# An encoder trunk in fp32 on one core: the next block's projections inside the attention units, conv groups between blocks, rotary halves swapped by DMA, 64-row scores

## The chip, the core and the metric

The kernel runs on one core of one Trainium2 chip. The metric is the device time of one launch in microseconds (us); lower is better. The engines are named as in the profile: PE (matrix engine; PEld is its weight load), DVE (vector engine), ACT (scalar engine), POOL (GpSimd), SP (the engine that issues most transfers).

## The reference

Two layers of an encoder on 1280 tokens (1024 of one sequence, 256 of another), 1024 wide. Each layer normalises its input, multiplies by `w_in`, and splits the 3072 result columns among three mixers. Their outputs together go through `w_out`, a norm and the residual; then a SwiGLU feed-forward network (2816 wide) with the same norms.

```python
hn = rmsnorm(x, g_pre_mix)
q_d, k_d, v_d, q_n, k_n, v_n, gate_b, gate_c, h_in = split(hn @ w_in)
y_dil  = dilated_attention(rope(q_d), rope(k_d), v_d)       # 6 heads of 64
y_na   = neighbourhood_attention(q_n, k_n, v_n, rpb)        # 4 heads of 64
y_conv = gate_b * conv3(gate_c * h_in)                      # 384 channels
x = x + rmsnorm(concat(y_dil, y_na, y_conv) @ w_out, g_post_mix)
hf = rmsnorm(x, g_pre_ffn)
x = x + rmsnorm((silu(hf @ w_gate) * (hf @ w_up)) @ w_down, g_post_ffn)
```

The three (window, dilation) pairs of the dilated attention are one softmax over all keys with the logarithm of a count added to the scores.

## The kernel before

**Precision.** Every product of two fp32 matrices is three matmuls on a high and a low part: high x high, high x low, low x high (`products`, L1617 to L1619). The high part is an ACT copy (`WH`, `XH`), the low part a subtraction on POOL (`WL`, L653) or DVE (`XL`).

**Tiling.** Activations lie transposed, features on the partitions, tokens in three chunks `c` of 512, 512 and 256 columns. A *group* is one 128-column slice of a weight matrix times one chunk: 8 k-tiles x 3 matmuls into one PSUM bank. A *weight unit* is that slice for all three chunks, such as `("k", 1)`.

**Attention blocks.** A block `b` holds two heads of 64, stacked in 128 partitions. Blocks 0 to 2 are dilated, 3 and 4 neighbourhood attention. Each has 20 *attention units* `u` (10 query tiles of 128 x 2 heads). The keys of a unit are 8 tiles (u 0 to 15) or 2 tiles (u 16 to 19) in dilated blocks, and 4, 5 or 2 tiles in the others. A unit passes through: `scores` on PE (L1730, L1731), `mask` on DVE (L1344: adds the table and gives the row maximum), `exp` on ACT (L921), `turn` on PE (L1742: transposes of the probabilities), their high part on ACT (`PTH`, L953) and low part on DVE (`PTL`, L1377), `values` on PE (L1763, L1764), `o_low` on ACT (`OT`, L931), `normalise` on DVE (`YN`, L1353), and for each second unit `turn_y` on PE (L1770) with `y_block` on ACT. Every engine works its instructions in the order in which they are written.

**Order around a block.** PE works the nine groups k, q, v of block `b`, then in blocks 0 to 2 the three `c` groups of the convolution; scores(0) and scores(1); `turn_v` (L1711: transposes of v); then the 20 units. In blocks 0 to 2 the `h` and `b` groups of the convolution are spread over units 0 to 11 (`convolution`). While PE works the projections, ACT and DVE make rotary embedding and the split into stacked halves.

**Rotary embedding.** `swap` on ACT copies four 32-row pieces of the group from PSUM to the exchanged place; DVE multiplies by sine and adds.

**Scores.** The contraction dimension is 64 per head. `QS[h]` holds the high part of q in one half of the 128 partitions and the low part in the other, `KH[h]` the high part of k twice. One 128-row matmul of `QS` with `KH` gives high x high and low x high, a second with `KL` the rest:

```python
nc.tensor.matmul(bank, q, KH[h][:, keys], start=True, stop=False)
last = nc.tensor.matmul(bank, q, KL[h][:, keys], start=False, stop=True)
```

**Banks.** Two results `o` of values use one bank (6) in dilated blocks and two (6 and 7, `out_banks`) in the others.

Of the kernel before, what the change touches and what calls it, by code (L numbers as in the profile page):

```python
# [54 lines left out]
MIXED_PIECES = ((0, 2), (2, 4), (5, 7), (7, 8))  # L55
VBANKS = ((6, 0, 4), (7, 4, 4), (6, 8, 2))
SUM_BANK = 7
CONV_PARTS = ((0, S_SAMPLE, 1), (S_SAMPLE, S_PROMPT, S_SAMPLE + 2))
# [40 lines left out]

def attention_weights(L):  # L100

    order = []
    for b in range(BLOCKS):
        order += [(L, part, b) for part in "kqv"]
        if b in DIL:
            order += [(L, part, b) for part in "chb"]
    return order + [(L, "o", i) for i in range(KT)]
# [19 lines left out]
NSLOT = 10  # L127
SPLIT = Numbered(WEIGHTS)
# [11 lines left out]


def conv_groups(L, b, parts):
    return [(L, part, b, c) for part in parts for c in range(NCH)]
# [21 lines left out]
def groups():  # L165
    order = first_block(0)
    for L in range(DEPTH):
        for b in range(BLOCKS):
            if b:
                order += [(L, part, b, c) for part in "kqv" for c in range(NCH)]  # L170
            if b in DIL:
                order += conv_groups(L, b, "chb")
# [23 lines left out]
def drains():  # L196
    order = []
    for L in range(DEPTH):
        for b in range(BLOCKS):
            order += first_block(L) if b == 0 else [(L, p, b, c) for p in "kqv" for c in range(NCH)]  # L200
            if b in DIL:
                order += conv_groups(L, b, "chb")
    return order
# [4 lines left out]
SWAP, SINE, ROPE = Numbered(ROPED), Numbered(ROPED), Numbered(ROPED)  # L208


def splits():

    order = []
    for L in range(DEPTH):
        for b in range(BLOCKS):
            if b == 0:
                order += [(L, p, b, c) for c in range(NCH) for p in "kq"]
            else:
                order += [(L, p, b, c) for p in "kq" for c in range(NCH)]
    return order  # L220


STACK_HI, STACK_LO = Numbered(splits()), Numbered(splits())


# [56 lines left out]
ON_VECTOR = [(2 * L + 1, "x", 0) for L in range(DEPTH - 1)]  # L282
# [14 lines left out]
def constants():  # L297
# [14 lines left out]
    eye_ones = np.concatenate([np.eye(P, dtype=f), np.ones((P, P), f), cmask], 1)  # L312
    return np.ascontiguousarray(np.concatenate([cos128, sin128, log], 1)), eye_ones


def build(nc, xt, w_in, w_out, w_gate, w_up, w_down, gains, conv_w, rpb, tables, small, mixed,
          parked, out):
    with ExitStack() as ctx:
# [19 lines left out]
        EYE = place("EYE", [P, 2 * P + GRID_W])  # L338
        ident, ones, cmask = EYE[:, 0:P], EYE[:, P:2 * P], EYE[:, 2 * P:]
# [9 lines left out]
                [base + o for o in (91136, 57344, 65536, 73728, 32768)]  # L349
# [5 lines left out]
        QS = [place(f"QS{h}", [P, T], F32R, offset=base + 5120 * h) for h in range(2)]  # L355
        KH = [place(f"KH{h}", [P, T], F32R, offset=base + 10240 + 5120 * h) for h in range(2)]
        KL = [place(f"KL{h}", [P, T], F32R, offset=base + 20480 + 5120 * h) for h in range(2)]
        V = place("V", [P, TILES, 2, P], F32R, offset=base + 30720)
        PR = place("PR", [P, 2, 1024], offset=base + 40960)
        pt = (w_at + 4 * 8192, base + 49152)  # L360
        PTH = [place(f"PTH{i}", [P, 2, 4, P], F32R, offset=o) for i, o in enumerate(pt)]
        PTL = [place(f"PTL{i}", [P, 2, 4, P], F32R, offset=o + 4096) for i, o in enumerate(pt)]
        TA = place("TA", [P, T + 4], offset=base + 57344)
        TB = place("TB", [P, T + 4], offset=base + 62496)
        TC = place("TC", [P, T + 4], offset=base + 67648)
        YB = place("YB", [P, T], offset=base + 72800)
        TAB = place("TAB", [P, 2 * T + 1920], offset=base + 77920)
        COS, SIN, LOG = TAB[:, 0:T], TAB[:, T:2 * T], TAB[:, 2 * T:]
        EB = place("EB", [P, 2, 14, GRID_W], offset=base + 77920)
        IB = place("IB", [P, 2, 10, GRID_W], offset=base + 85088)  # L370
        STAT = place("STAT", [P, 16], offset=base + 95840)
        NM, SM, RC, CW = STAT[:, 0:4], STAT[:, 4:8], STAT[:, 8:12], STAT[:, 12:15]
        OT = place("OT", [P, 2, HD], offset=base + 95904)
        YN = place("YN", [P, 2, P], offset=base + 96416)
# [3 lines left out]
              for c, o in enumerate((0, 16384, 82944))]  # L378
        ACC = [place(f"ACC{c}", [P, KT, n], offset=base + KT * t0 * 4) for c, (t0, n) in enumerate(CHUNKS)]
        SQ = {k: place(f"SQ{k}", [P, 2, 512], offset=base + o) for k, o in (("y", 40960), ("x", 45056))}  # L380
        SS2 = place("SS2", [P, 256], offset=base + 81920)
        SS = {k: place(f"SS{k}", [P, 512], offset=base + o) for k, o in (("y", 49152), ("x", 51200))}
        RT = [place(f"RT{i}", [P, 512], offset=base + 53248 + 2048 * i) for i in range(2)]
        HH = [place(f"HH{t}", [P, T], F32R, offset=base + 57344 + 5120 * t) for t in range(2)]
        HL = [place(f"HL{t}", [P, T], F32R, offset=base + 67584 + 5120 * t) for t in range(2)]
        HF = [place(f"HF{t}", [P, T], offset=base + 67584 + 5120 * t) for t in range(2)]
        SG = place("SG", [P, T], offset=base + 77824)
# [25 lines left out]
        s_tabs = sem("tabs")  # L413
        s_sine = sem("sine")
        s_rope = sem("rope")
# [7 lines left out]
        s_mask_may = sem("mask_may")  # L423
# [10 lines left out]
        s_ylo = sem("ylo")  # L434
        s_edge = sem("edge")
        s_gated = sem("gated")
        s_tap = sem("tap")
        s_convolved = sem("convolved")
# [51 lines left out]

        def span(c):
            return slice(CHUNKS[c][0], CHUNKS[c][0] + CHUNKS[c][1])
# [5 lines left out]
        def _(sp):  # L498
# [23 lines left out]
            def load_tables(L):  # L522
                sp.dma_start(TAB[:, 0:2 * T], tables[:, 0:2 * T]).then_inc(s_tab, 16)
                sp.dma_start(LOG, tables[:, 2 * T:]).then_inc(s_log, 16)
# [21 lines left out]
            def biases(L, j):  # L546
                sp.wait_ge(s_masked, NU * (BLOCKS * L + 3 + j))
# [20 lines left out]
            for L in range(DEPTH):  # L568
                for b in DIL:
                    if b:  # L570
                        load((L, "h", b))
                    load((L, "b", b))
                    taps(L, b)
                    for part in "kqv":
                        load((L, part, b + 1))
                    load((L, "c", b + 1) if b < 2 else (L, "k", 4))
                biases(L, 0)
                load((L, "q", 4))
                load((L, "v", 4))
                load((L, "o", 0))  # L580
                biases(L, 1)
                for i in (1, 2, 3):
                    load((L, "o", i))

                sp.wait_ge(s_group, GROUP[L, "v", 4, 2])
                sp.wait_ge(s_yout, 16 * 4 * (L + 1))
                sp.wait_ge(s_cout, 16 * 3 * (L + 1))
                for c, (t0, n) in enumerate(CHUNKS):
                    for b0, b1 in ((0, LAST), (LAST + 1, KT)):
                        sp.dma_start(X[c][:, b0:b1, :], mixed[b0:b1, :, t0:t0 + n]  # L590
                                     .rearrange("b p n -> p b n")).then_inc(s_mload[c], 16)

                sp.wait_ge(s_stack_lo, STACK_LO[L, "q", 4, 2])
                sp.wait_ge(s_vt, 3 * (BLOCKS * L + 5))
                load((L, "o", 4))
# [1392 lines left out]
```

## Time and profile before

| | |
|---|---|
| median of 3 runs | 3641.13 us (3640.95 to 3644.62) |
| the profiled execution | 3638.91 us, span 3636.3 us |
| mean granted clock of PE | 0.964 |
| attention of layer 0 (start to last value) | 732.5 us, of layer 1 about 714 us |
| PE busy | 94% of the span |

The span is from the first to the last instruction; 2.6 us of the time lie around it. The attention ends of the two layers are where the last `turn_y` of block 4 stands in the timeline (732.4 and 2545 us; layer 1 begins at 1831). Matmuls are pipelined, so what a matmul costs PE is the distance from its start to that of the next, not its duration.

### The profile page before, as it was taken

To read this page: it belongs to the slowest core of one execution; us is meant where nothing else is said; L and a number is where in the kernel's file an instruction comes from. 1 tells how busy PE (TensorE), PEld (TensorE's weight loads), DVE (VectorE), ACT (ScalarE), POOL (GpSimd) and SP (SyncE) were. 2 spreads that over 40 slices of the span, in tenths; PEclk is the share of its full clock that TensorE was granted. 3 is DMA by queue.
4 is the path that set the end of the run, shared out by engine and by line. 5 is a ranking of instruction groups with operands and counts; after the bars stand their busy time and mean duration, and the time that the engine had idled before them with its cause. 6 is when DMAs were issued, how large, how long until landed. Compare 5 with 4: busy or idle time off the path is not lost. (4 is left out here: it accounts for less than half of the span.)

```text
span 3636.3 us, 45371 instructions
## 1 busy us (share of the span) xinstructions
PE 3414.5 (94%) x18616; PEld 2936.7 (81%) x18616; DVE 1517.9 (42%) x2862; ACT 1157.1 (32%) x2254; POOL 908.9 (25%) x566
## 2 busy tenths in 40 slices
PE   6899998998999999999878999998989999999997
PEld 5788887777888888888767788877878888888886
DVE  3555445525223333322665554555152333332225
ACT  5445445624111111111344454446241111111112
POOL 4101010325322222222431010103252222222223
PEclk8999999999999999999989999999999999999998
DMA  3010111213111111111310100112121111111112
GB/s 126 12 44 13 38 37 36 80 44 119 47 41 35 41 35 35 37 46 35 124 64 12 38 20 31 43 30 86 58 99 53 35 41 35 35 36 47 35 35 116
DMA packets 43341, 179.67 MB, mean 49 GB/s; under 512 B 5376, under 2 KB 7296, under 8 KB 39552
## 3 DMA queue, kind: packets, MB, share of 16 engines
q1 hardware_dynamic: 41120, 167.60, 13.5%
q10 hardware_dynamic: 2016, 9.18, 0.6%
q8 instruction: 148, 2.42, 0.3%
q14 instruction: 57, 0.47, 0.0%
HBM read 146.61 MB, written 30.15 MB: 49 GB/s over the span
## 5 line engine op out<-in xcount | busy, mean ns | idle before, releaser
L1617 PE MATMUL PS<-XH,WH 128*128 128x512 f32 (+1 forms) x3648 | 1321.3, 362 | 30.3 <-DVE XL L1250 13.5
L1618 PE MATMUL PS<-XL,WH 128*128 128x512 f32 (+1 forms) x3648 | 1312.0, 360 | 0.0
L1619 PE MATMUL PS<-XH,WL 128*128 128x512 f32 (+1 forms) x3648 | 1311.4, 359 | 0.0
L1617 PEld LDWEIGHTS PS<-XH,WH 128*128 128x128 f32 x3648 | 702.7, 193 | 136.7 <-POOL WL L653 16.1
L653 POOL TENSOR_TENSOR WL<-RAW,WH 128x1024 fp32r<-128x1024 f32 x196 | 470.3, 2419 | 1269.9 <-ACT WH L820 1269.8
L1618 PEld LDWEIGHTS PS<-XL,WH 128*128 128x128 f32 x3648 | 701.6, 192 | 101.6
L1619 PEld LDWEIGHTS PS<-XH,WL 128*128 128x128 f32 x3648 | 700.2, 192 | 102.9
L676 POOL TENSOR_TENSOR SG<-SG,RS 128x512 f32<-128x512 f32 x132 | 147.6, 1118 | 1015.8 <-ACT SG L987 1015.8
L1428 DVE TENSOR_TENSOR ACC<-ACC,PS 128x512 f32<-128x512 f32 (+1 forms) x480 | 286.4, 598 | 252.3 <-PE PS L1619 250.5
L1617 PE MATMUL PS<-HH,WH 128*128 128x512 f32 (+1 forms) x1056 | 378.6, 358 | 11.3 <-DVE ACC L1428 9.8
L987 ACT ACTIVATE SG<-SG 128x512 f32<-128x512 f32 x132 | 73.9, 560 | 975.5 <-DVE SG L1406 975.3
L1619 PE MATMUL PS<-HH,WL 128*128 128x512 f32 (+1 forms) x1056 | 380.9, 361 | 0.0
L1618 PE MATMUL PS<-HL,WH 128*128 128x512 f32 (+1 forms) x1056 | 378.7, 359 | 0.0
L1763 PE MATMUL PS<-V,PTH 128*128 128x128 f32 x1136 | 276.2, 283 | 25.5 <-issue 14.7
L1764 PE MATMUL PS<-V,PTL 128*128 128x128 f32 x1136 | 278.1, 285 | 0.0
L1406 DVE TENSOR_TENSOR SG<-PS,RS 128x512 f32<-128x512 f32 x132 | 79.4, 602 | 450.7 <-PE PS L1619 445.9
L1763 PEld LDWEIGHTS PS<-V,PTH 128*128 128x128 f32 x1136 | 228.6, 201 | 40.8 <-issue 21.2
L1412 DVE TENSOR_TENSOR HF<-PS,SG 128x512 f32<-128x512 f32 x132 | 79.5, 602 | 415.6 <-PE PS L1619 401.9
L1617 PEld LDWEIGHTS PS<-HH,WH 128*128 128x128 f32 x1056 | 200.0, 189 | 44.2 <-DVE ACC L1428 11.1
L1377 DVE TENSOR_TENSOR PTL<-PS,PTH 128x512 fp32r<-128x512 f32 (+1 forms) x328 | 190.9, 614 | 96.9 <-ACT PTH L953 94.6
L1764 PEld LDWEIGHTS PS<-V,PTL 128*128 128x128 f32 x1136 | 229.2, 202 | 2.5
L1618 PEld LDWEIGHTS PS<-HL,WH 128*128 128x128 f32 x1056 | 200.3, 190 | 33.7
(105 smaller groups left out, 3459.6 us busy)
## 6 DMA issues: line engine op xcount, KB each, us to landing
RAW<-w_in SPq DMA_DIRECT2D x48, 512.0 KB, 3.6
RAW<-w_gate SPq DMA_DIRECT2D x44, 512.0 KB, 3.6
RAW<-w_up SPq DMA_DIRECT2D x44, 512.0 KB, 3.6
RAW<-w_down SPq DMA_DIRECT2D x44, 512.0 KB, 3.8
X<-parked SPq DMA_DIRECT2D x6, 2048.0 KB, 7.2
RAW<-w_out SPq DMA_DIRECT2D x16, 512.0 KB, 3.7
parked<-YO SPq DMA_DIRECT2D x4, 2048.0 KB, 6.9
mixed<-YB ACTq DMA_DIRECT2D x8, 640.0 KB, 2.9
```

What stands on the lines that cost most here:

```text
L653: nc.gpsimd.tensor_tensor(WL[s][:, :, :], RAW[s][:, :, :], WH[s][:, :, :].bitcast(F32), ALU.subtract).then_inc(s_lo, 1)
L676: nc.gpsimd.tensor_tensor(SG[:, span(c)], SG[:, span(c)], RS[:, span(c)], ALU.mult) \
L987: nc.scalar.activation(SG[:, span(c)], SG[:, span(c)], ACT.Silu) \
L1377: nc.vector.tensor_tensor(PTL[u % 2][:, g, 0:n, :].rearrange("p t q -> p (t q)"), PS[:, 4 + g, 0:n * P], high.bitcast(F32), ALU.subtract) \
L1406: nc.vector.tensor_tensor(SG[:, span(c)], PS[:, bank_of(L, "g", f, c), 0:CHUNKS[c][1]], RS[:, span(c)], ALU.mult).then_inc(s_gate, GATE.st ...
L1412: nc.vector.tensor_tensor(HF[f % 2][:, span(c)], PS[:, bank_of(L, "u", f, c), 0:CHUNKS[c][1]], SG[:, span(c)], ALU.mult).then_inc(s_h, HID ...
L1428: ins = nc.vector.tensor_tensor(ACC[c][:, k, :], ACC[c][:, k, :], ps, ALU.add)
L1617: nc.tensor.matmul(out, wh, xh, start=first, stop=False)
L1618: nc.tensor.matmul(out, wh, xl, start=False, stop=False)
L1619: return nc.tensor.matmul(out, wl, xh, start=False, stop=last)
L1763: nc.tensor.matmul(o, PTH[u % 2][:, g, j, :], v, start=a + j == 0, stop=False)
L1764: last = nc.tensor.matmul(o, PTL[u % 2][:, g, j, :], v, start=False, stop=a + j == nkt - 1)
```

## The change

**Scores.** q and k are kept once, high and low (`QH`, `QL`, `KH`, `KL`), each head in its own 64 partitions. `scores` now serves a pair of units (both heads of a query tile): per 512 keys three matmuls of 64 rows for each head, head 0 and head 1 in turn, into different banks.

**Fill.** The projections k, q, v of block `b+1` are worked between the units of block `b` (`FILL`, `fill_steps`); block 4 has only the `b` groups of the last convolution. One unit of weights before each block (`COVER`: `c`, `c`, `b`, `c`, `h`) is worked around its start: its first chunk inside the last unit of the block before, the two others after `turn_v`. The splits of block `b+1` stand in units 18 and 19 of block `b` on ACT and DVE.

**Rotary.** `swap` is now four transfers of 32 rows from SBUF to SBUF on SP's queue for each group, into one buffer `SW`; DVE does sine, cosine and sum. The first block, whose q and k are not spread over units, uses the same path.

**Also.** `values` uses one bank (6) in all blocks. The splits of the mixers' outputs of chunks 1 and 2 move from block 4 into the output projection. In the first norm the adds of chunk 1's squares move from POOL to DVE, and ACT works that norm in another order. The memory places of many buffers move.

```diff
+COVER = (("c", 0), ("c", 1), ("b", 1), ("c", 2), ("h", 2))
+FILL = ((("h", 0), ("k", 1), ("q", 1), ("v", 1), ("b", 0)),
+        (("k", 2), ("q", 2), ("v", 2), ("h", 1)),
...
+        (("b", 2),))
+FILL_FROM = (0, 0, 0, 0, 1)
+FILL_WIDTH = ((1,) * 15, (1,) * 12, (1, 1) + (2,) * 7, (2,) * 9, (3,) * 3)
...
-            def swap(L, part, b, c):
-
-                act.wait_ge(s_drained, DRAIN[L, part, b, c])
...
-                    nc.scalar.activation(TC[32 * o:32 * o + 32, span(c)], ps[32 * q:32 * q + 32, :],
-                                         ACT.Copy).then_inc(s_swap, 1)
+            def swap(L, part, b, c):
+
+                n = CHUNKS[c][1]
+                key = (L, part, b, c)
+                sp.wait_ge(s_drained, DRAIN[key])
+                if SWAP[key] > 1:
+                    sp.wait_ge(s_rope, SWAP[key] - 1)
+                SWAP.step(key)
+                for q in range(4):
+                    o = q ^ 1
+                    sp.dma_start(SW[32 * o:32 * o + 32, 0:n], RAW_OF[part][32 * q:32 * q + 32, span(c)]) \
+                        .then_inc(s_swap, 16)
...
+                nc.vector.tensor_tensor(SW[:, 0:n], SW[:, 0:n], SIN[:, span(c)], ALU.mult) \
+                    .then_inc(s_sine, SINE.step(key))
+                nc.vector.tensor_tensor(raw, raw, COS[:, span(c)], ALU.mult) \
+                    .then_inc(s_cosine, COSINE.step(key))
                 dve.wait_ge(s_sine, SINE[key])
+                dve.wait_ge(s_cosine, COSINE[key])
+                nc.vector.tensor_tensor(raw, raw, SW[:, 0:n], ALU.add).then_inc(s_rope, ROPE.step(key))
...
                     for a, n in quads(nkt):
                         keys = slice((k0 + a) * P, (k0 + a + n) * P)
-                        bank = PS[:, 2 * (u % 2) + a // 4, 0:n * P]
-                        nc.tensor.matmul(bank, q, KH[h][:, keys], start=True, stop=False)
-                        last = nc.tensor.matmul(bank, q, KL[h][:, keys], start=False, stop=True)
-                    last.then_inc(s_scored, 1)
+                        for m, (q, k) in enumerate(((QH, KH), (QH, KL), (QL, KH))):
+                            for h in range(2):
+                                own = slice(HD * h, HD * h + HD)
+                                last = nc.tensor.matmul(PS[:, 2 * h + a // 4, 0:n * P],
+                                                        q[own, i * P:(i + 1) * P], k[own, keys],
+                                                        start=m == 0, stop=m == 2)
+                                if m == 2 and a + n == nkt:
+                                    last.then_inc(s_scored, 1)
...
+                turn_v(nb)
+                cover(L, b, 1)
+                cover(L, b, 2)
+                pe.wait_ge(s_vl, 3 * nb + 3)
                 scores(0)
-                scores(1)
-                turn_v(nb)
                 for u in range(NU):
                     turn(u)
-                    if u == 0:
-                        pe.wait_ge(s_vl, 3 * nb + 3)
-                    if u + 2 < NU:
-                        scores(u + 2)
-                    if beside is not None:
-                        beside(u, 0)
+                    if u % 2 == 0 and u + 2 < NU:
+                        scores(u // 2 + 1)
+                    fill(u, 0)
                     if u >= 3 and u % 2:
                         turn_y(u // 2 - 1)
-                    if beside is not None:
-                        beside(u, 1)
+                    fill(u, 1)
+                    if u == NU - 1 and b != LAST:
+                        cover(L, b + 1, 0)
                     if u:
                         values(u - 1)
                 values(NU - 1)
```

PE at the end of block 0 before the change: the last unit's `turn`, `turn_y`, the values of units 18 and 19, the last `turn_y`, and the first group of block 1.

```order
L1742 MATMUL PS<-EYE,PR 128x128 [waits ptl,exped]
...
L1770 MATMUL PS<-EYE,YN 128x128 [waits y]
L1763 MATMUL PS<-V,PTH_102 128x128 [waits ptl,yb,y]
...
L1763 MATMUL PS<-V,PTH_103 128x128 [waits ptl,yb,y]
...
L1770 MATMUL PS<-EYE,YN 128x128 [waits y]
```

The same place after the change (`Rv` is the raw v of block 1, `WH_64` the weights of the cover unit `("c", 1)`).

```order
L1723 MATMUL PS<-EYE,PR 128x128 [waits ptl,exped]
...
L1749 MATMUL PS<-EYE,YN 128x128 [waits y]
L1600 MATMUL PS<-XH_49,WH_64 128x512 [waits lo]
...
L1742 MATMUL PS<-V,PTH_102 128x128 [waits ptl,yb,y]
...
L1742 MATMUL PS<-V,PTH_103 128x128 [waits ptl,yb,y]
...
L1749 MATMUL PS<-EYE,YN 128x128 [waits y]
L1685 MATMUL PS<-EYE,Rv 128x128 x10
```

One cover group has come between `turn_y` and the last two values, and `turn_v` of the next block stands right behind the last `turn_y`.

DVE at the same place after the change (L1389 is `PTL`, L1331 the low parts of k and q of block 1, L1398 and L1377 reciprocal and `normalise`). Before the change the low parts of k and q stood behind the projections of block 1, and nothing stood between `PTL`, the reciprocal and `normalise`.

```order
L1389 TENSOR_TENSOR PTL_104<-PS,PTH_102 128x256 [waits pth]
L1331 TENSOR_TENSOR KL<-Rk,KH 128x512 [waits stack_hi]
L1331 TENSOR_TENSOR QL<-Rq,QH 128x512 [waits stack_hi]
L1331 TENSOR_TENSOR KL<-Rk,KH 128x512 [waits stack_hi]
L1398 RECIPROCAL STAT<-STAT 128x1 [waits exped]
L1377 SCALAR_TENSOR_TENSOR YN<-PS,STAT,OT 128x64 [waits o_tmp]
L1389 TENSOR_TENSOR PTL_105<-PS,PTH_103 128x256 [waits pth]
L1331 TENSOR_TENSOR QL<-Rq,QH 128x512 [waits stack_hi]
L1331 TENSOR_TENSOR KL<-Rk,KH 128x256 [waits stack_hi]
L1331 TENSOR_TENSOR QL<-Rq,QH 128x256 [waits stack_hi]
L1398 RECIPROCAL STAT<-STAT 128x1 [waits exped]
L1377 SCALAR_TENSOR_TENSOR YN<-PS,STAT,OT 128x64 [waits yt,o_tmp]
```

Three subtractions have moved ahead of the `normalise` of unit 17, and three ahead of that of unit 18.

## Rows read from the trace of the kernel before

**Rows 1.** The page: span, and busy time of PE.
```profile
span 3636.3 us, 45371 instructions
PE 3414.5 (94%) x18616; PEld 2936.7 (81%) x18616; DVE 1517.9 (42%) x2862; ACT 1157.1 (32%) x2254; POOL 908.9 (25%) x566
```
**Rows 2.** Waits of PE: us in total, times, longest us.
```profile
PE PS L1730 <- DVE TA L1287: 28.3, 6, 15.9
...
PE PS L1711 <- DVE V L1327: 17.7, 10, 3.0
```
**Rows 3.** Timeline, PE, scores of an 8-tile unit (start us, us).
```profile
145.38 0.40 PE L1731 MATMUL PS<-KL,QS 128*128 128x512 f32 x1
...
146.08 0.28 PE L1617 MATMUL PS<-XH,WH 128*128 128x256 f32 x1
146.19 0.28 PE L1618 MATMUL PS<-XL,WH 128*128 128x256 f32 x1
```
**Rows 4.** Timeline, layer 0 up to its first block, DVE, PE and POOL.
```profile
47.50 0.69 DVE L1287 TENSOR_TENSOR TB<-PS,TAB 128x512 f32<-128x512 f32 x1
...
60.38 5.99 POOL L664 TENSOR_TENSOR SSx<-SSx,SQx 128x256 f32<-128x256 f32 x7
...
115.52 0.33 PE L1742 MATMUL PS<-EYE,PR 128*128 128x128 f32 x1 [0.59 <-ACT PR L921]
```
**Rows 5.** Timeline, layer 1 up to its first block, DVE, ACT and PE.
```profile
1865.98 0.69 DVE L1287 TENSOR_TENSOR TB<-PS,TAB 128x512 f32<-128x512 f32 x1 [0.20 <-DVE TAB L1260]
...
1873.09 1.99 ACT L820 ACTIVATE WH<-RAW 128x1024 fp32r<-128x1024 f32 x2
...
1925.36 0.48 PE L1742 MATMUL PS<-EYE,PR 128*128 128x128 f32 x1 [1.88 <-ACT PR L921]
```
**Rows 6.** Small transfers: issues (KB each, median us to landing), four in a row.
```profile
mixed<-YB ACTq DMA_DIRECT2D x8, 640.0 KB, 2.9
...
STAT<-conv_w SPq DMA_DIRECT2D x6, 1.5 KB, 3.4
...
524.49 2.46 SPq L551 DMA_DIRECT2D EB<-rpb  x4
```
**Rows 7.** Timeline, first unit of block 1, DVE and ACT.
```profile
270.49 1.23 DVE L1344 CUSTOM_DVE_ANT_0 PR<-PS,TAB 128x1024 f32<-128x1024 f32 x1 [1.49 <-PE PS L1731]
...
272.17 0.59 ACT L910 ACTIVATE V<-PS 128x512 fp32r<-128x512 f32 x1
272.65 1.15 ACT L921 ACTIVATE PR<-PR,STAT 128x1024 f32<-128x1024 f32 x1
```
**Rows 8.** Timeline, last units of block 0, PE and DVE.
```profile
205.12 0.41 PE L1742 MATMUL PS<-EYE,PR 128*128 128x128 f32 x2
...
209.60 0.28 DVE L1353 SCALAR_TENSOR_TENSOR YN<-PS,STAT,OT 128x64 f32<-128x64 f32 x1 [1.53 <-ACT OT L931]
...
211.91 0.78 PE L1617 MATMUL PS<-XH,WH 128*128 128x512 f32 x1
```
**Rows 9.** Windows: busy PE, PEld, DVE, ACT, POOL; granted clock; DMA share, GB/s.
```profile
205.00:212.00 7.00, 4.24 (x22) 3.22 (x21) 2.12 (x8) 2.75 (x10) 0.00 (x0) 0.70 0.24 96
212.00:219.00 7.00, 7.00 (x27) 5.66 (x27) 0.00 (x0) 0.28 (x1) 0.00 (x0) 0.81 0.23 94
...
577.00:583.00 6.00, 2.58 (x18) 1.80 (x16) 5.21 (x13) 2.88 (x6) 0.00 (x0) 1.00 0.20 75
583.00:590.00 7.00, 6.28 (x27) 5.63 (x26) 3.89 (x13) 3.72 (x9) 0.00 (x0) 0.52 0.00 0
```
**Rows 10.** Timeline, block 3: DVE at its start, PE at its end.
```profile
575.94 2.02 DVE L1519 TENSOR_TENSOR EB<-EB,EYE 128x1792 f32<-128x1792 f32 x1
...
579.80 0.69 DVE L1344 CUSTOM_DVE_ANT_0 PR<-PS,EB 128x512 f32<-128x512 f32 x1 [0.21 <-DVE IB L1526]
...
626.43 0.33 PE L1742 MATMUL PS<-EYE,PR 128*128 128x128 f32 x1 [0.45 <-ACT PR L921]
...
630.77 0.56 PE L1617 MATMUL PS<-XH,WH 128*128 128x512 f32 x1
```

More of the change, by code:

```diff
@@ L899, in split_q @@
-            def split_q(L, b, c):
-                ready(L, "q", b, c)
-                nc.scalar.activation(QS[0][0:64, span(c)], TA[0:64, span(c)], ACT.Copy)
-                nc.scalar.activation(QS[1][64:128, span(c)], TA[64:128, span(c)], ACT.Copy) \
-                    .then_inc(s_stack_hi, STACK_HI.step((L, "q", b, c)))
-            def split_v(nb, parts):
-                for g in parts:
-                    bank, a, n = VBANKS[g]
+                    act.wait_ge(s_drained, DRAIN[key])
@@ new lines, in split @@
+                if part == "k" and c == 0:
+                    if b:
+                        act.wait_ge(s_scored, NU * (BLOCKS * L + b))
+                    else:
+                        act.wait_ge(s_xl, XLO[2 * L - 1, "x", 2, KT - 1])
+                        for cc in range(NCH) if L else ():
+                            act.wait_ge(s_zst[cc], 16 * 2 * L)
+                dst = KH if part == "k" else QH
+                nc.scalar.activation(dst[:, span(c)], RAW_OF[part][:, span(c)], ACT.Copy) \
+                    .then_inc(s_stack_hi, STACK_HI.step(key))
@@ L908, in split_v @@
+            def split_v(nb):
+                for g, (bank, a, n) in enumerate(VBANKS):
                     act.wait_ge(s_vt, 3 * nb + g + 1)
@@ L1328, in split_v, with attention @@
                                             ALU.subtract).then_inc(s_vl, 1)
-            def attention(L, b, table, beside=None):
+            def attention(L, b, table, beside):
                 nb = BLOCKS * L + b
                 units, starts, tp = units_of(b), quad_starts(units_of(b)), TP_BASE[nb]
-                banks, first = out_banks(b), NU * nb
+                first = NU * nb
                 def mask(u):
@@ new lines, in _ @@
+                    for part in "kqv":
+                        drain(L, part, 0, c)
+                    for part in "kq":
+                        rope(L, part, 0, c)
+                    if c:
+                        for cc in (0, 1) if c == 1 else (2,):
+                            low(L, "k", 0, cc)
+                            low(L, "q", 0, cc)
+                for b in range(BLOCKS):
+                    nb = BLOCKS * L + b
+                    steps = fill_steps(L, b)
+                    cover = cover_groups(L, b)
+                    drain(*cover[0])
+                    split_v(nb)
+                    drain(*cover[1])
+                    drain(*cover[2])
+                    if b == 0:
+                        dve.wait_ge(s_sq, SQUARE[2 * L - 1, "x", 2, KT - 1])
+                        if L:
+                            dve.wait_ge(s_zst[2], 16 * 2 * L)
+                        for col in (0, S_SAMPLE + 1, T + 2):
+                            nc.vector.memset(TC[:, col:col + 1], 0.0).then_inc(s_edge, 1)
+                        dve.wait_ge(s_log, 16 * (L + 1))
+                    if b not in DIL:
```

765 lines of the change are left out of this document (337 added, 428 removed), and 4 rows, old and new, of the table SPLIT_BESIDE.

## The prediction

> **What bounds the kernel now.** The page first: PE is busy 94% of the span [rows 1], so the time is what PE has to stream plus what it loses. Then the waits of PE: its longest single one in the attention stage is scores waiting for the last step of q (28.3 us in 6 waits, one of them 15.9), the next `turn_v` waiting for bank 6 (17.7 in 10) [rows 2]. Then the timeline, block by block. The reader is to see that PE does not wait in the middle of a dilated block, filled or not: it waits in front of the first block of a layer, at each block's end, where units of two key tiles follow each other and one result bank serves them, and at each block's start. The windows last: after such a stretch the granted clock is 0.70, 0.81 or 0.52 of full speed, that is, partly at 1.2 GHz instead of 2.4 [rows 9], and dense work pays for that.
>
> The projections that the change moves into the units are dense PE work in either place. Moving them gains only where they cover a wait, and takes cover away from what stood beside them.
>
> **Scores.** Three steps from 145.38 to 146.08 are 0.70 us, so a 512-column matmul costs PE 0.233 us, a 256-column one 0.11 to 0.12 [rows 3]. An 8-tile unit costs 4 x 0.233, a pair of units 1.87. After the change a pair is 12 matmuls of 64 rows. No row of before shows one. If the two heads run at once, it is 6 x 0.233 = 1.40, 0.47 less; there are 48 such pairs: -22 us. The 16 pairs of 4 tiles give -4, the 16 of 5 tiles nothing, and the 20 of 2 tiles +4, since I take each of its six weight loads at the 0.11 of the smallest step in these rows, which is more than four 256-column matmuls cost. Sum -22. If every matmul takes its own turn, the same counts give +45, +7, +11 and +5: +68. Between 128-row and 64-row matmuls PE changes over 200 times. A change costs between nothing and what a matmul's duration exceeds its spacing, 0.40 - 0.23 = 0.17 us [rows 3]: 0 to +33. I take +10, nearer to nothing, since the steps up to 146.08, where PE goes over from scores to a projection, show no pause. I take both at once: -22 + 10 = **-12**.
>
> The Trainium skill, "TensorE: Matmul & The Clock Gate", Part 3 on packing small matmuls, says that matmuls on different row groups run concurrently, a few ns apart. By that page alone the term would be -22. The skill's "TensorEngine Tiling (Array Packing)", Key Properties, says that changing the tiling mode drains the engine, which speaks against this change: by it the term would lie near the upper end of the change-over bound, +11. No run here shows either yet.
>
> **Start of a layer.** In the first block the chain is what counts, not PE. A group of q or k now goes: DVE drain (0.69 us for 512 columns [rows 4]), four transfers, three DVE steps (2.1, for 256 columns 1.3), and the next group's transfers start only then. Small transfers land 2.9 to 3.4 us after issue, and four in a row take 2.46 us to issue, 0.6 apart [rows 6]. So a swap takes between 2.9 (all at once) and 3.4 + 1.85 = 5.3; I take 4.4, with an issue each 0.3 to 0.4 us for pieces this small.
>
> *Layer 0.* The sum of chunk 1's squares loses its wait on POOL, and the scale of chunk 1 is there near 60 us (squares of chunk 2 take 6 us for seven adds [rows 4] and stand ahead of it on ACT). The chain starts at 47.5 as before [rows 4]: k and q of chunk 0 end at 60.7, three drains, k and q of chunk 1 at 74.4, four low parts 77.2, drains 78.4, k and q of chunk 2 at 89.1, low parts, first cover drain and low parts of v at 92.6. PE's own work up to there ends near 88, so scores(0) starts at 92.7. From it to the first `turn`: 1.2 us to head 0's last matmul, 0.55 until the mask starts, mask 1.23 and 0.1, exp 1.15 and 0.2 [rows 7]: 97.1. Before it was 115.5 [rows 4]: -18, of which I give 2 back for the clock. *Layer 1.* The two table steps before the first drain (1865.98 [rows 5]) are gone: 1863.4. The same chain ends at 1909, the scale of chunk 1 (behind two weight copies that end at 1875.1 [rows 5]) being early enough. First `turn` at 1914 to 1915 against 1925.4 [rows 5]: -11, with the clock -9. Together **-25**. Ten swaps lie on these chains, so the bounds of 2.9 and 5.3 move the sum by -15 and +9.
>
> **Ends of blocks.** From `turn` of unit 18 to the next dense group were 6.8 us in block 0 (205.12 to 211.91 [rows 8]). After the change DVE's `normalise` of unit 17 stands behind three low parts (0.69 each) which wait for three ACT copies (0.59 each [rows 7]), and these stand behind `o_low` of unit 17. `turn_y` waits for it, and behind `turn_y` PE's cover group: 3.3 us of wait. The cover group (24 x 0.233 = 5.6) runs; then values(18), `o_low`, three copies, three low parts, `normalise` (3 us), values(19), `o_low`, `normalise` (0.28 after its release [rows 8]), `turn_y`. Counted from `turn` of unit 18: 15.5 us, without the cover group 9.9. That is +3.2 at each end of blocks 0, 1, 2. Block 3 took 4.3 us with its two result banks (626.43 to 630.77 [rows 10]) and now has one: +5.5. Block 4 has no splits behind it, but one bank: +1. Both layers: 2 x (9.6 + 5.5 + 1) = **+32**. Queued behind the waiting `turn_y` is all of PE; behind DVE's low parts the reciprocal and `normalise`. Bounds: nothing, if the copies come earlier than I read, and +45 at double the DVE time.
>
> **Clock.** Before, an end leaves 7 us at 0.81 (1.3 us lost in dense work), and an NA start 7 us at 0.52 [rows 9]. After, the cover group follows 5 us of thin work, and the next `turn_v` and cover follow 4 more: I count 2 us more at each of eight ends, and 1.5 at four starts of dilated blocks: **+22**, between 0 and +40.
>
> **Starts of blocks.** Dilated: nothing covers mask and exp of unit 0 any more, 2.9 us instead of 2.3. Neighbourhood: the bias steps hold the mask until 3.9 us after they begin (575.94 to 579.80 [rows 10]), as before: +0.4. Eight starts: **+4**. `turn_v` itself now waits for nothing, and v's low parts hide beside the cover groups (8.4 us of PE).
>
> **Rest.** Block 3 is filled to unit 17, which hides its waits for exp such as the 0.45 at 626.43 [rows 10]; I count 3 us a layer, with block 4: **-6**. In block 4 units 10 to 19 stay bare, now with one result bank: **+5**. At nothing: rope in the units (DVE needs 5.9 us of 8.9, and a swap lands a unit later; without this cover 1 to 2 us a group), the ACT splits moved into the output projection (6 us in 44), weight loads on SP behind swaps (each at least three units early), taps and gates. Should one load be late, the unit behind waits some 3 us once, the landing of a small transfer [rows 6].
>
> **Sum.** -12 - 25 + 32 + 22 + 4 - 6 + 5 = +20 against 3638.9 of the profiled execution, which lies 2.2 below the median of the runs: 3661 on the scale of the median.
>
> **Rivals.**
> *The block ends do not get longer* (the other side). If the copies and low parts slip into time in which `normalise` waits anyway, and the cover group keeps PE's clock, terms three and four vanish: -54, 3607. For it: `normalise` already waited 1.53 us for ACT at that place [rows 8], and DVE is busy only 2.1 of 7 us [rows 9]. Against: the low parts stand ahead of it in order and wait for copies that start only after `o_low` of unit 17. It decides where ends and clock together cost under 3.4 us for each of ten block ends.
> *The clock holds.* Only the fourth term vanishes: 3639, no change. For it: the window with the wait itself, 577 to 583, is still at 1.00 [rows 9]. Against: the stretches get longer, and 0.52 followed a wait of 3 us [rows 9].
> *64-row matmuls take turns.* +68 instead of -22: 3751. For it: no row shows two matmuls at once. Against: nothing ties the heads together but the bank, and these differ.
>
> **How the numbers follow.** Forecast 0.40; ends not longer 0.22; clock holds 0.15; turns 0.17; something not seen 0.06. The forecast's own spread is the change-over, the swap and the clock, about 25 us down and 30 up. 3597 to 3702 holds all but the turn-taking and some of the edges. 0.2% (7 us) is about what a measurement can tell. Faster: 0.22, 0.04 of the forecast and 0.04 of the rest, 0.30. Same: half of the clock case and 0.06 more, 0.13. Slower: 0.57.
>
> **What would show it.** Scores: starts of the two heads' matmuls in the timeline under 0.05 us apart, pairs 0.23 apart. Starts: first `turn` near 97 and 1914. Ends: a wait of about 3 us in front of the `turn_y` ahead of the cover group, another behind it before values(19). Clock: windows over cover groups below 0.8. I am wrong if the waits at the ends are under 2 us, if the pair costs 12 steps, or if a swap takes over 6 us.

## The result, and the profile after

The changed kernel takes 3654.6 us (median of 6 runs, 3652.3 to 3661.97), the kernel before 3642.7 beside it (6 runs). The ratio is 1.0035, with a 95% interval of 1.0023 to 1.0048: slower by 12 us. The profiled execution took 3652.3 us (3638.91 before). One of the five executions of the kernel with two banks, further down, took 6336 us; it counts in that kernel's median and not in its ratio. In the rows below `turn` is L1723, `scores` L1707, `turn_y` L1749, `values` L1742 and L1743, `turn_v` L1685; on DVE `low` is L1331, `normalise` L1377.

The page, span and busy time:
```profile
span 3650.5 us, 45904 instructions
PE 3423.3 (94%) x18944; PEld 2921.6 (80%) x18944; DVE 1459.7 (40%) x2741; ACT 1015.1 (28%) x1996; POOL 913.1 (25%) x577
```
DVE and ACT together have 200 us less work than before [rows 1]. PE sets the time, and it is busy 9 us longer than before. The waits of PE (us in total, times, longest):
```profile
PE PS L1723 <- ACT PR L966: 36.4, 12, 5.2
PE PS L1749 <- DVE YN L1377: 34.8, 34, 2.8
PE PS L1742 <- DVE YN L1377: 26.2, 20, 2.6
...
PE PS L1685 <- DVE Rv L1301: 8.7, 2, 7.2
...
PE PS L1723 <- DVE PTL L1389: 4.9, 2, 2.4
```
The long wait of scores in front of the first block [rows 2] is gone. In its place stand three kinds: `turn`(0) of each block for its exp, `turn_y` and `values` at the ends of blocks for `normalise`. They are one row each here, so the next views are timelines. PE at the end of block 0, from `turn` of unit 18 on:
```profile
226.61 0.41 PE L1723 MATMUL PS<-EYE,PR 128*128 128x128 f32 x2
...
231.50 0.48 PE L1749 MATMUL PS<-EYE,YN 128*128 128x128 f32 x1 [2.66 <-DVE YN L1377]
231.63 0.78 PE L1600 MATMUL PS<-XH,WH 128*128 128x512 f32 x1
...
241.69 0.47 PE L1742 MATMUL PS<-V,PTH 128*128 128x128 f32 x1 [2.57 <-DVE YN L1377]
...
243.79 0.42 PE L1685 MATMUL PS<-EYE,Rv 128*128 128x128 f32 x1
```
DVE in the same place:
```profile
229.29 0.69 DVE L1331 TENSOR_TENSOR KL<-Rk,KH 128x512 fp32r<-128x512 f32 x1 [1.40 <-ACT KH L948]
229.90 0.68 DVE L1331 TENSOR_TENSOR QL<-Rq,QH 128x512 fp32r<-128x512 f32 x1
230.50 0.68 DVE L1331 TENSOR_TENSOR KL<-Rk,KH 128x512 fp32r<-128x512 f32 x1
231.10 0.15 DVE L1398 RECIPROCAL STAT<-STAT 128x1 f32<-128x1 f32 x1
231.18 0.26 DVE L1377 SCALAR_TENSOR_TENSOR YN<-PS,STAT,OT 128x64 f32<-128x64 f32 x1
```
`normalise` of unit 17 stands behind three low parts, and 0.3 us after its start PE moves again. The end takes 17.2 us from 226.61 to 243.79, cover group included, against 6.8 before [rows 8]. The windows (us, busy PE, PEld, DVE, ACT, POOL, granted clock, DMA share, GB/s) over that end, over the next block's first cover, and over the two halves of block 4:
```profile
226.60:231.50 4.90, 1.76 (x11) 1.12 (x11) 3.06 (x11) 3.25 (x9) 0.00 (x0) 0.62 0.09 33
231.50:238.50 7.00, 7.00 (x25) 5.75 (x26) 0.27 (x1) 0.28 (x1) 0.00 (x0) 0.78 0.01 2
...
243.80:250.80 7.00, 7.00 (x28) 6.07 (x28) 1.98 (x4) 1.75 (x4) 1.27 (x1) 0.68 0.23 94
...
672.60:715.90 43.30, 40.26 (x297) 34.49 (x298) 25.34 (x73) 25.13 (x64) 7.79 (x5) 1.00 0.27 95
715.90:737.70 21.80, 17.78 (x77) 14.15 (x76) 7.73 (x31) 13.64 (x35) 16.62 (x9) 0.50 0.25 92
```
The first cover group runs at 0.78, the next block's at 0.68, and the last 22 us of block 4 at 0.50, all of it at 1.2 GHz. These are its bare units, with nothing between them to fill PE. Before, the same units ran at 0.96:
```profile
702.00:732.50 30.50, 24.84 (x181) 21.37 (x179) 20.05 (x74) 26.65 (x72) 20.62 (x12) 0.96 0.06 19
```
Scores of an 8-tile pair in block 0 (PE; x2 are two matmuls that start together):
```profile
128.39 0.82 PE L1723 MATMUL PS<-EYE,PR 128*128 128x128 f32 x6
129.14 0.50 PE L1707 MATMUL PS<-KH,QH 64*128 64x512 f32 x2
129.48 0.40 PE L1707 MATMUL PS<-KL,QH 64*128 64x512 f32 x2
...
130.40 0.39 PE L1707 MATMUL PS<-KH,QL 64*128 64x512 f32 x2
130.73 0.50 PE L1600 MATMUL PS<-XH,WH 128*128 128x512 f32 x1
131.07 0.40 PE L1601 MATMUL PS<-XL,WH 128*128 128x512 f32 x1
```
Both heads run at once. The six matmuls of `turn` are 0.11 us apart, so the last starts at 128.94. From there to the second projection matmul are 2.13 us, and 0.11 + 6 x 0.233 + 0.233 would be 1.74. The 0.39 us between the two is what going from 128-row matmuls to 64-row ones and back costs; the experiments below test that. I call one such change of form a change-over. Last the starts of the layers, PE, then SP and DVE in the first swap:
```profile
94.42 0.90 PE L1723 MATMUL PS<-EYE,PR 128*128 128x128 f32 x3 [2.71 <-ACT PR L966]
1914.45 0.90 PE L1723 MATMUL PS<-EYE,PR 128*128 128x128 f32 x3 [2.71 <-ACT PR L966]
```
```profile
47.65 2.50 SPq L561 DMA_DIRECT2D SW<-Rk  x4
```
```profile
51.67 0.69 DVE L1318 TENSOR_TENSOR SW<-SW,TAB 128x512 f32<-128x512 f32 x1 [2.85 <-DMA SW<-Rk]
```
This first swap takes 4.0 us from issue to use; the other five in front of the first block take 3.7 to 3.85. The first `turn` comes 21.1 us earlier in layer 0, and 10.9 in layer 1 though that layer starts 3.2 later: 35 us for both.

### The profile page after: what moved, and what is told of

It is laid out like the page before. It is cut to its first block and busy times, and to the rows that moved or that the text cites. A ratio compares the mean times of both kernels' runs of the same rounds, so it can differ in the third digit from the quotient of the medians.

```text
span 3650.5 us, 45904 instructions
## 1 busy us (share of the span) xinstructions
PE 3423.3 (94%) x18944; PEld 2921.6 (80%) x18944; DVE 1459.7 (40%) x2741; ACT 1015.1 (28%) x1996; POOL 913.1 (25%) x577
## 5 line engine op out<-in xcount | busy, mean ns | idle before, releaser
L1600 PE MATMUL PS<-XH,WH 128*128 128x512 f32 (+1 forms) x3648 | 1347.0, 369 | 22.3 <-DVE XL L1276 13.2
L1742 PE MATMUL PS<-V,PTH 128*128 128x128 f32 x1136 | 270.7, 279 | 42.6 <-DVE YN L1377 26.2
L1743 PE MATMUL PS<-V,PTL 128*128 128x128 f32 x1136 | 275.5, 283 | 0.0
L1742 PEld LDWEIGHTS PS<-V,PTH 128*128 128x128 f32 x1136 | 225.1, 198 | 60.5 <-DVE YN L1377 31.1
L1389 DVE TENSOR_TENSOR PTL<-PS,PTH 128x512 fp32r<-128x512 f32 (+1 forms) x328 | 191.1, 615 | 126.5 <-ACT PTH L994 125.7
L1743 PEld LDWEIGHTS PS<-V,PTL 128*128 128x128 f32 x1136 | 226.8, 200 | 3.7
```

Of the source, the lines that this page charges most:

```text
L1389: nc.vector.tensor_tensor(PTL[u % 2][:, g, 0:n, :].rearrange("p t q -> p (t q)"), PS[:, 4 + g, 0:n * P], high.bitcast(F32), ALU.subtract) \
L1600: nc.tensor.matmul(out, wh, xh, start=first, stop=False)
L1742: nc.tensor.matmul(o, PTH[u % 2][:, g, j, :], v, start=a + j == 0, stop=False)
L1743: last = nc.tensor.matmul(o, PTL[u % 2][:, g, j, :], v, start=False, stop=a + j == nkt - 1)
```

## Experiments

Each edit is made to the changed kernel (3654.6); `...` in an edit marks lines left out. All kernels ran beside the kernel before, which stayed at 3642.6 to 3642.7; ratios are to it.

**The order at the block ends.** DVE's low parts of k and q go behind `normalise`:
```diff
                     if u < NU:
-                        beside(u)
+                        if u < 18 or b == LAST:
+                            beside(u)
...
                     if 1 <= u <= NU:
                         normalise(u - 1)
+                    if 18 <= u < NU and b != LAST:
+                        beside(u)
```


> The changed kernel, with the six low parts of the next block's k and q behind `normalise` of units 17 and 18 on DVE instead of ahead of it; nothing else moves. If the order on DVE makes the block ends long, both waits there (2.66 us before `turn_y` ahead of the cover group, 2.57 before values(19)) go, at eight ends: -42 us, and the clock after them gives back another 5 to 10: 3603 to 3612 against 3654.6. If the ends are long for the one result bank and the thin work itself, the waits only move behind the copies on ACT or to scores(0), which needs the low parts: less than 15 us gained, 3640 or more.


Measured: 3609.5 us, ratio 0.9911 (0.9897 to 0.9925), 45 us less. Its waits of PE (here `turn_y` is L1752, `values` L1745):
```profile
PE PS L1752 <- DVE YN L1377: 18.5, 34, 1.1
...
PE PS L1745 <- DVE YN L1377: 10.7, 20, 0.7
```
61.0 us of waiting for `normalise` became 29.2. Both long waits went and nothing took their place: the eight ends are 39 us shorter together, so the order of DVE's steps was the cause. This edit alone turns the change from slower to faster than before.

**Two runs of scores instead of one.** In filled units the two halves of the keys are apart:
```diff
...
-                        scores(u // 2 + 1)
-                    fill(u, 0)
+                        scores(u // 2 + 1, 0)
+                        fill(u, 0, 1)
+                        scores(u // 2 + 1, 1)
+                        fill(u, 0, 2)
```


> The changed kernel, with the scores of an 8-tile pair in two runs of six 64-row matmuls instead of one of twelve, the first tile of the filled group between them, in the units that are filled. That is two change-overs more in some 38 pairs. If a change of the row group's size costs about 0.19 us, as the spacing around the runs reads (a pair takes 1.79 us, six slots of 0.233 would be 1.40), this is +14 to +15 us: 3669. If the 0.39 us of a pair is something else, such as the wait for the masks that the run begins with, it is not paid twice: within 4 us of 3654.6.


Measured: 3674.2 us, ratio 1.0088 (1.0075 to 1.0102), 20 us more. The second run of such a pair on PE:
```profile
130.89 0.40 PE L1602 MATMUL PS<-XH,WL 128*128 128x512 f32 x1
131.22 0.50 PE L1709 MATMUL PS<-KH,QH 64*128 64x512 f32 x2
131.55 0.40 PE L1709 MATMUL PS<-KL,QH 64*128 64x512 f32 x2
131.78 0.40 PE L1709 MATMUL PS<-KH,QL 64*128 64x512 f32 x2
132.12 0.50 PE L1600 MATMUL PS<-XH,WH 128*128 128x512 f32 x1
132.45 0.39 PE L1601 MATMUL PS<-XL,WH 128*128 128x512 f32 x1
```
A slot is the time from one matmul's start to the next. Without its neighbours' slots a run of six matmuls takes 1.10 us, three slots and 0.39; a pair takes 2.2 instead of 1.79. In 40 pairs that is +16, so the 0.39 us is paid once for each run. The other 4 us were not traced.

**The 64-row form priced.** Half as many matmuls of 128 rows. This kernel leaves out half of the products of each score, so it shows only what the form costs:
```diff
-                        for m, (q, k) in enumerate(((QH, KH), (QH, KL), (QL, KH))):
-                            for h in range(2):
-                                own = slice(HD * h, HD * h + HD)
...
+                        for h, m, q, k in ((0, 0, QH, KH), (0, 1, QL, KH), (1, 2, QH, KL)):
```


> The changed kernel, with each run of scores made of half as many matmuls of 128 rows (6 instead of 12 for 8 tiles), over both heads at once: head 0's bank gets two of them, head 1's one. The scores are other numbers (they mix the heads and leave half of the products out), so this only prices the 64-row form: the same number of slots of PE, and no change of the row group. If the extra 0.39 us of a pair (1.79 instead of 6 x 0.233) is the change-over and nothing else, 100 pairs give back 0.35 to 0.39 each: -35 to -39 us, 3616 to 3620. If it comes from the weight loads or the order of the banks, it stays: less than 8 us gained.


Measured: 3608.7 us, ratio 0.9912 (0.9898 to 0.9925), 46 us less. PE in the same pair, whose six matmuls take six slots and nothing more:
```profile
126.21 0.48 PE L1705 MATMUL PS<-KH,QH 128*128 128x512 f32 x1
...
127.45 0.40 PE L1705 MATMUL PS<-KL,QH 128*128 128x512 f32 x1
127.69 0.40 PE L1600 MATMUL PS<-XH,WH 128*128 128x512 f32 x1
127.92 0.40 PE L1601 MATMUL PS<-XL,WH 128*128 128x512 f32 x1
```
By the runs of each size 34 us go, about what was expected. The other 12 are more, and which stretch gave them was not separated. This edit also halves the number of matmuls and weight loads; the kernel with two runs keeps their number and still pays 0.39 us for each run more. The two together show that the change-overs are the price.

**Three apart, six apart.** Head 0's three matmuls of a bank ahead of head 1's, and then all six:
```diff
-                        for m, (q, k) in enumerate(((QH, KH), (QH, KL), (QL, KH))):
-                            for h in range(2):
+                        for h in range(2):
+                            for m, (q, k) in enumerate(((QH, KH), (QH, KL), (QL, KH))):
```


> The changed kernel, with the three matmuls of head 0 issued ahead of the three of head 1, where before they alternate; same counts, same banks. If two matmuls of 64 rows run at once only when they stand next to each other in PE's order, an 8-tile pair loses four of its six overlaps (only the third of one head and the first of the other meet): 12 slots become 12 less 2 or so, about 10 x 0.233 instead of 6, +0.9 us for 48 pairs, +0.2 to +0.5 for the 52 others: +60 us, 3715. If PE takes matmuls of the other row group ahead of waiting ones, nothing changes: 3655.


Measured: 3656.5 us, ratio 1.004 (1.0025 to 1.0056), no difference from 3654.6. The expected serialisation did not come: pairs start together as before, though three matmuls lie between the partners in the order of issue.
```profile
128.33 0.40 PE L1707 MATMUL PS<-KH,QH 64*128 64x512 f32 x2
128.56 0.40 PE L1707 MATMUL PS<-KL,QH 64*128 64x512 f32 x2
```
```diff
-                    for a, n in quads(nkt):
...
+                    for h in range(2):
+                        for a, n in quads(nkt):
```


> The changed kernel, with all of head 0's scores (both halves of the keys, six matmuls) issued ahead of head 1's. Three ahead cost nothing (3656.5 against 3654.6). If PE runs the two row groups as two streams however far apart they are issued, six cost nothing either: 3655. If it looks only some instructions ahead, the last ones of head 1 run alone: for each of 48 pairs of 8 tiles up to three slots of 0.233, +10 to +35 us.


Measured: 3697.0 us, ratio 1.0154 (1.014 to 1.0167), 42 us more. PE in the same pair:
```profile
129.12 0.50 PE L1707 MATMUL PS<-KH,QH 64*128 64x512 f32 x1
129.46 0.39 PE L1707 MATMUL PS<-KL,QH 64*128 64x512 f32 x1
129.70 0.39 PE L1707 MATMUL PS<-KH,QL 64*128 64x512 f32 x1
129.70 0.61 PE L1707 MATMUL PS<-KH,QH 64*128 64x512 f32 x2
...
130.97 0.39 PE L1707 MATMUL PS<-KH,QL 64*128 64x512 f32 x1
131.29 0.50 PE L1600 MATMUL PS<-XH,WH 128*128 128x512 f32 x1
```
Head 1's first matmul, the seventh issued, starts at 129.70 with head 0's third, 0.22 us ahead of the fourth; before that head 0 runs alone, at the end head 1. A pair takes 0.58 us more, a pair of five tiles 0.57: 64 of them are +37 of the 42, a little over the +35 that was expected at most.

**A second result bank where it is free.**
```diff
...
+def bk(b, u):
+    return FILL_BANK if u % 2 and u > last_fill(b) else Y_BANK
...
-                    o = PS[:, Y_BANK, 0:P]
+                    o = PS[:, own, 0:P]
```


> The changed kernel, with the results of odd units in bank 7 as soon as the block's last filled group is drained (units 15 on in block 0, 12 on in block 1, 16 on in block 2, 18 on in block 3, 10 on in block 4). If the single result bank is what block 4 and the ends lose, half of the idle time in block 4's last ten units goes (some 4 us a layer), 0.5 us for each bare unit of the others, and the clock with it: -12 to -25 us, 3630 to 3642. If these units wait for mask and exp instead, the bank is worth under 4 us.


Measured: 3627.1 us, ratio 0.9955 (0.9942 to 0.9969), 27 us less, a little over what was expected. In the timeline each of the eight ends is 1.3 to 2.1 us shorter (14 together), block 4 from `turn` 0 on 2.9 us a layer (6). The rest fits dense work at a higher clock (0.964 over the span of the profiled execution instead of 0.958), but was not separated.

**Scores(0) ahead of the last cover group.**
```diff
...
                 cover(L, b, 1)
-                cover(L, b, 2)
                 pe.wait_ge(s_vl, 3 * nb + 3)
                 scores(0)
+                cover(L, b, 2)
```


> The changed kernel, with scores(0) of each block ahead of the cover group of chunk 2 instead of behind it, so that mask and exp of unit 0 run beside 24 matmuls of 256 columns (2.8 us); on DVE the drain of chunk 2 goes behind mask(1), and in the neighbourhood blocks the bias steps go ahead of the drain of chunk 1. If the waits of `turn`(0) for exp (2.6 us in six blocks, 5.2 and 4.8 in four) are only a matter of order, they go but for some tenths: -15 at the dilated blocks, at least -11 at the others: 3625 to 3630. If they come back in front of the first filled group (behind mask(1) on DVE) or scores(1), the gain is under 8 us: 3647 or more.


Measured: 3619.4 us, ratio 0.9937 (0.9925 to 0.9949), 35 us less, where 25 to 30 were expected. `turn`(0) waits for nothing in blocks 1 to 4 of both layers; from `turn_v` to `turn`(0) block 4 takes 12.0 us instead of 17.5, block 3 13.1 instead of 17.1. Block 0's start takes 2 us more: scores(0) now comes ahead of a cover group and waits longer for the low parts of v (5.7 and 3.0 us in the two layers, against 2.8 and nothing). Elsewhere the waits did not come back.

**Two swaps in flight.**
```diff
...
+                into = TA if (part, b) == ("q", 0) else SW
...
-                    sp.dma_start(SW[32 * o:32 * o + 32, 0:n], RAW_OF[part][32 * q:32 * q + 32, span(c)]) \
+                    sp.dma_start(into[32 * o:32 * o + 32, 0:n], RAW_OF[part][32 * q:32 * q + 32, span(c)]) \
```


> The changed kernel, with q's halves of the first block swapped into TA (free at that time) instead of into the one buffer SW, so that the swaps of k and q of a chunk are in flight together. Each chunk's chain gets shorter by the landing of one swap, about 2 us of some 13. If the chain of swaps still sets the first `turn`, layer 1 gains most of its 7.2 us in front of `turn_v` (three chunks, -6) and layer 0 up to 3: -6 to -9, 3646 to 3649. If PE's own work and the statistics of chunk 2 set it by now, it is under 2 us.


Measured: 3647.0 us (11 runs, 3637.2 to 3653.7), ratio 1.0005 (0.9995 to 1.0016): 8 us less. Four of the runs lie at 3637 to 3638 and seven at 3646 to 3654, and nothing here tells why, so the 8 us are less sure than the other gains. The wait in front of layer 1's `turn_v` falls from 7.2 to 3.1 us, and layer 0's first `turn` comes at 90.05 instead of 94.42. The chain of swaps had set both.

**Block 4 filled longer.**
```diff
-FILL_WIDTH = ((1,) * 15, (1,) * 12, (1, 1) + (2,) * 7, (2,) * 9, (3,) * 3)
+FILL_WIDTH = ((1,) * 15, (1,) * 12, (1, 1) + (2,) * 7, (2,) * 9, (4,) * 3)
...
-                        if b == LAST and 12 <= u < 17:
-                            mixed_high(L, 0, u - 12)
+                        if b == LAST and 15 <= u < 20:
+                            mixed_high(L, 0, u - 15)
```


> The changed kernel, with the three groups that fill units 1 to 9 of block 4 spread over units 1 to 12, and the copies of the mixed pieces three units later (units 15 to 19). If block 4's second half is long for the clock (27 us at 1.2 GHz from 716 on, where the kernel before ran the same thin units at 2.4 GHz), the stretch at the low clock gets shorter: -4 to -8 us a layer, 3639 to 3647. If the bare units wait only for their own chain, nothing is gained, and the later copies may cost the output projection up to 3 us a layer: 3655 to 3661.


Measured: 3655.4 us, ratio 1.0041 (1.0028 to 1.0053), no gain. Its profiled execution is the slowest of the five (3666.9), so only its shape is read. The end of block 4 grows from 7.5 to 11.1 us in both layers; the copies on ACT come later there, which may be the reason. The low clock stayed (30.7 us at 1.2 GHz from 721 on, against 27.3 from 716 on). So this edit does not settle what the clock alone would give, and why these units fall to 1.2 GHz now and did not before stays open.

**All four, and the taps.** The edits of low parts, banks, scores(0) and swaps together:


> The edits of the four kernels together: low parts last, odd units' results in bank 7 where it is free, scores(0) ahead of the last cover group, two swaps in flight. Low parts last gave -45 us and two banks -27, which overlap at the eight ends by about 10; scores early is expected at -25 and the swaps at -8. If the waits are separate: -90 to -95, 3560 to 3565. If each uncovers another (ACT's splits behind PE's thin work, DVE at the block starts): -65, 3590.


Measured: 3538.7 us, ratio 0.9715 (0.9702 to 0.9729). That is 116 us less than the changed kernel; alone the four gave 45, 27, 35 and 8, 115 together. The waits were separate, and the overlap of 10 us that was expected at the ends did not come. One that remained is `turn`(1) of block 4, so:
```diff
...
-                        if b == LAST and u == 0:
-                            tap(L, 2, 0)
-                            tap(L, 2, 1)
-                        if b == LAST and u == 1:
-                            tap(L, 2, 2)
+                        if b == LAST and u < 3:
+                            tap(L, 2, u)
```


> The kernel with the four edits together (3538.7), and with the three tap steps of the last convolution in units 0, 1 and 2 of block 4 instead of two in unit 0 and one in unit 1. In its profile `turn`(1) of block 4 waits 2.79 us behind two taps on DVE that take 0.9 and 3.5 us. If the taps make that wait, a layer gains 0.9 to 2 us (the long one stays, alone in its unit), 3535 to 3537; if the second tap simply delays unit 2 as much, nothing: 3539. If the first filled group then waits for the scaled taps, it is slower by up to 2 us.


Measured: 3524.5 us, ratio 0.9684 (0.967 to 0.9699), 14 us less again, where the expectation was 2 to 4. The wait of 2.79 us is gone in both layers (5.6 us), and two waits of 0.55 in front of filled groups, whose drain stands behind the scaled taps, are new. In the profiled executions block 4 from `turn` 0 to `turn` of unit 18 takes 60.6 us instead of 65.0, and the stretch to the first down projection 3.5 us less in the one layer, 3.8 in the other, with less of it at 1.2 GHz. That is 16 us for 4.5 us of waiting, so there the clock gave more than the wait. The size is less sure than the sign: the four runs of the one kernel span 7 us and the five of the other 14, and these two profiled executions lie 22 us apart instead of 14. The bare units at the end of block 4 are still at 1.2 GHz. This version beats both kernels.

## Why the prediction was right, step by step

Slower was forecast with a chance of 0.57, at 3661; it is 3654.6. The terms are set below beside what the two profiled executions show (the length of each stretch in both, less the slots of PE that moved in or out of it, 0.2265, 0.115 and 0.109 us for 512, 256 and 128 columns):

| term | predicted | measured |
|---|---|---|
| scores | -12 | +2 |
| starts of the layers | -25 | -35 |
| block ends, with two thirds of the clock term | +32 + 16 | +51 |
| starts of blocks 1 to 4, with the rest of it | +4 + 6 | +1 |
| middle of blocks 3 and 4 | -6 + 5 | -14 + 9 |
| middle of blocks 0 to 2 | 0 | +4 |
| output projection and after | 0 | -3 |
| sum | +20 | +15 (the spans differ by 14) |

The direction, and the ends with their clock that make it, came as forecast. That the sum is only 5 us off is partly luck: scores are 14 us worse than forecast, the starts of the layers 10 better, the starts of the blocks 9 better, and the others miss by 3 to 8 either way.

*Scores.* "A change costs between nothing and ..." 0.17, taken at 0.05: this is the step that was mis-sized, and past its own bound. A change costs 0.19, 200 of them 38 us instead of 10. By size: 48 pairs of 8 tiles went from 1.87 to 1.79 us (-4), 16 of 4 tiles from 0.84 to 1.06 (+3.5), 16 of 5 tiles from 1.22 to 1.37 (+2.4). The 20 of 2 tiles went from 0.36 to between 0.70 and 0.75 where nothing waits, +7 at most; most stand where PE waits anyway, and the table leaves them in the other terms. Without the change-overs the packing was worth some 6 us more than the -22 forecast; with that and the 7 us left out the term is off by 14, though the change-overs alone were off by 28. The reasoning that the steps up to 146.08 show no pause was beside the point, since both sides of that step have 128 rows. The Trainium skill, "TensorEngine Tiling (Array Packing)", Key Properties, says that a change of tiling mode drains the engine. The trace and the run with full rows agree with that: 0.39 us for two changes, and none when all runs have 128 rows. That the heads run at once was right.

*Starts of the layers.* The chain was right. In layer 0 the first `turn` came 2.7 us ahead of the forecast. It was not the swaps of the first two chunks: those took 3.85 to 4.0 us instead of 4.4, but the three DVE steps behind them took 2.1 to 2.8 instead of 2.1, and chunk 1 ended only 0.4 ahead. Most of the rest came in chunk 2, whose transfers left at 76.8, right behind the drain of k, and not behind all three drains at 78.4. The issues of a swap are 0.6 us apart, not the 0.3 to 0.4 that was taken for small pieces. In layer 1 it came where it was forecast, though the layer began 3.2 us later. The 4 us given back for the clock were not lost.

*Ends.* 3.3 and 3 us of wait were predicted, 2.66 and 2.57 measured; with the clock the eight ends cost 47 us against 46 predicted (19 + 11 + 16), block 4's 3.5 against 2. The run with the low parts last shows the cause: it takes 39 of these 47 us away.

*Clock.* Windows over the cover groups were forecast below 0.8: 0.78 and 0.68. At the dilated starts 1.5 us more were forecast, and none came on top of what the dense group behind an end had lost before [rows 9]. The forecast missed the second half of block 4, at 0.50, and no run shows what brings it about.

*Blocks 3 and 4.* Block 3's filled units hid more than forecast (-7 us a layer, not some -3). Block 4 cost 9 instead of 5. Units 10 to 17 take 26.3 us instead of 18.3 in each layer: the one bank is worth 2.6 of these 8 (2.9 with the end, against 3.5 predicted), and the rest was not separated; the clock, 0.73 there instead of 1.00, and the 64-row scores lie in it. The first ten units gave 2 us back a layer, though two taps in unit 0, which the prediction counted "at nothing", hold `turn`(1) for 2.44 us.

*Rivals.* Matmuls taking turns is excluded by their starts, "the clock holds" by the windows, "ends not longer" by the waits; the kernel with the low parts last is close to what that rival describes, and at 3609.5 it lies near its 3607. The clock over its first cover groups is still 0.71 to 0.79 in six of eight, so part of that nearness is chance. The 35 us gained at the layers' starts and the 14 in block 3 were there, and the ends took 51 of them back, by the place of six short steps.

## What to carry to other kernels

Where independent copies are tucked into an engine's stream beside a tight chain, they go behind the step that the other engine waits for: the same six low parts cost 45 us more ahead of it than behind it. A gain that packing small matmuls promises has to be set against each change of form, here 0.39 us for each run. The 0.47 us gained in the longest runs hardly pays for it, and the shorter runs do not pay. Where waits repeat at every block boundary, their fixes added up (115 us alone, 116 together), and the last small wait gave back more than it lasted, through the clock as far as two traces can tell.

## What was not expected of the hardware

- Two streams on different rows of PE are not held to the order of issue. With three matmuls between partners nothing was lost. With six the seventh matmul started ahead of the fourth, and still 0.58 us of a pair was lost. The Trainium skill, "TensorE: Matmul & The Clock Gate", Part 2 (step by step), says that only weight loads are pulled ahead and that matmuls stay in program order; the starts in this trace differ (129.704 for the seventh, 129.927 for the fourth), and the measurement decides. The sentence in the section on the kernel before, that every engine works its instructions in the order in which they are written, does not hold for these either.
- The same step on DVE took 3.56 us beside a step on POOL and 1.54 without one. In the changed kernel, block 4, DVE (taps two and three) and POOL:
```profile
668.25 3.56 DVE L1345 SCALAR_TENSOR_TENSOR TA<-TC,STAT,TA 128x1281 f32<-128x1281 f32 x1
...
672.99 1.54 DVE L1345 SCALAR_TENSOR_TENSOR TA<-TC,STAT,TA 128x1281 f32<-128x1281 f32 x1
```
```profile
667.45 3.00 POOL L721 TENSOR_TENSOR WL<-RAW,WH 128x1024 fp32r<-128x1024 f32 x1 [43.83 <-ACT WH L884]
```
In all twelve traces of the changed kernel and its variants the ten such steps of a run without a POOL step beside them take 1.54 to 1.56 us. The second tap of block 4, in both layers, took 3.54 to 3.56 with an overlap of 2.2 us in eleven of them. In the kernel with the taps in three units the overlap is 0.99, and the step took 2.34. So the step lasts longer by nearly the time that the two overlap. That is a regularity over one place in the kernel; no run varied it by itself.
